# Two experts' token rows selected by one-hot products on TensorE in a two-layer transformer step on one Trainium2 core

## The reference, cut to what matters

```python
def hier_moe(h, w_rg_l, w_re_l, w_gate_l, w_up_l, w_down_l):
    grp_logits = jnp.einsum('btd,dg->btg', h, w_rg_l)              # 4 groups
    grp_idx = jnp.argmax(grp_logits, axis=-1)
    ...                                                            # the 4 experts of that group
    top_val, top_idx = lax.top_k(exp_logits, TOP_K)                # TOP_K = 2
    gates = ...                                                    # 16 experts, two not zero per token
    hidden = jax.nn.silu(jnp.einsum('btd,edf->btef', h, w_gate_l)) * jnp.einsum('btd,edf->btef', h, w_up_l)
    hidden = hidden * gates[..., None]
    return jnp.einsum('btef,efd->btd', hidden, w_down_l)           # f = 256, d = 1024
```

## Time and profile before

| what | value |
|---|---|
| median of 3 runs | 1436.62 us (1427.18 to 1441.4) |
| profiled execution, its own time | 1429.83 us |
| its span, first to last instruction | 1428.1 us |
| mean granted TensorE clock | 0.939 of 2.4 GHz |
| PE busy | 1253.6 us (88%) |
| DVE, ACT, POOL busy | 537.6, 378.2, 155.8 us |
| share of the ending chain on PE, DMA, DVE | 78%, 7%, 6% |

### The profile page before, as it was taken

How to read it: one execution, slowest core, us unless ns; L and a number is a source line. 1 busy time by engine, 2 the same in 40 slices (tenths; PEclk the granted TensorE clock), 3 DMA queues, 4 the chain that set the end, 5 groups by cost and what they waited for, 6 DMA issues and landing times.

```text
span 1428.1 us, 16575 instructions
## 1 busy us (share of the span) xinstructions
PE 1253.6 (88%) x5768; PEld 721.4 (51%) x5768; DVE 537.6 (38%) x1371; ACT 378.2 (26%) x963; POOL 155.8 (11%) x257
## 2 busy tenths in 40 slices
PE   4999897899999869999689998789999996999970
PEld 2455454465566545444355555456556653445430
DVE  0232264445565422112143415454546542111216
ACT  0121254434333101111021215453433310111111
POOL 3200210100000210000131102000000011000005
PEclk9999889999999979999899997999899997999995
DMA  9986635699111688999862143531001168799945
GB/s 347 391 303 215 239 127 196 239 365 327 64 59 60 248 310 320 370 364 369 296 234 88 65 159 127 207 120 65 32 31 59 60 243 324 285 365 369 365 188 221
DMA packets 125355, 314.75 MB, mean 220 GB/s; under 512 B 9520, under 2 KB 57936, under 8 KB 112608
## 3 DMA queue, kind: packets, MB, share of 16 engines
q1 hardware_dynamic: 90160, 240.50, 46.6%
q0 software_dynamic: 13072, 47.07, 8.8%
q10 hardware_dynamic: 22048, 26.22, 5.2%
HBM read 233.05 MB, written 80.71 MB: 220 GB/s over the span
## 4 chain that ended last, share of the span: by engine, by line
PE 78%; DMA 7%; DVE 6%; issue 3%; ACT 2%; SPq 2%; POOL 1%; ACTq 0%; POOLq 0%; DVEq 0%
PE ps L705 16%; PE ps L781 15%; PE ps L638 10%; PE ps L461 9%; PE ps L801 8%; PE ps L521 7%; DMA ring<-in_w_mod 4%; PE ps L480 3%; PE ps L542 3%; PE ps L466 2%; PE ps L728 2%; SPq L869 1%; DMA big<-in_x 1%; PE ps L596 1%; PE ps L507 1%
## 5 line engine op out<-in xcount | busy, mean ns | idle before, releaser
L705 PE MATMUL ps<-ring,big 128*128 128x384 f32 (+2 forms) x640 | 232.3, 522 | 3.9 <-ACT big L1157 3.9
L705 PEld LDWEIGHTS ps<-ring,big 128*128 128x128 f32 x640 | 121.1, 191 | 107.2 <-issue 64.7
L781 PE MATMUL ps<-ring,arena 128*128 128x512 f32 x384 | 169.1, 593 | 2.4 <-DVE arena L1899 2.4
L521 PE MATMUL ps<-arena 64*128 64x128 f32 (+5 forms) x576 | 142.5, 454 | 21.5 <-DVEq L1601 14.2
L461 PEld LDWEIGHTS ps<-consts,arena 128*128 128x128 f32 (+2 forms) x888 | 110.5, 160 | 77.1 <-issue 52.8
L461 PE MATMUL ps<-consts,arena 128*128 128x128 f32 (+2 forms) x888 | 134.5, 283 | 14.6 <-ACT arena L1073 6.4
L638 PE MATMUL ps<-ring,big 128*128 128x512 f32 x320 | 143.0, 598 | 2.4 <-DVE arena L1667 1.6
L1073 ACT ACTIVATE arena<-ps 128x384 f32<-128x384 f32 (+3 forms) x140 | 69.0, 493 | 242.2 <-PE ps L461 241.8
L521 PEld LDWEIGHTS ps<-arena 64*128 64x128 f32 (+1 forms) x576 | 82.3, 210 | 80.8 <-issue 68.1
L781 PEld LDWEIGHTS ps<-ring,arena 128*128 128x128 f32 x384 | 71.2, 190 | 83.4 <-issue 83.4
L638 PEld LDWEIGHTS ps<-ring,big 128*128 128x128 f32 x320 | 59.0, 190 | 72.4 <-issue 66.4
(11 more groups left out here) (197 smaller groups left out, 1386.0 us busy)
## 6 DMA issues: line engine op xcount, KB each, us to landing
ring<-in_w_mod SPq DMA_DIRECT2D x20, 2048.0 KB, 14.2
ring<-in_w_up SPq DMA_DIRECT2D x22, 1024.0 KB, 8.6
ring<-in_w_gate SPq DMA_DIRECT2D x22, 1024.0 KB, 5.8
slots<-zeros ACTq DMA_DIRECT2D x8, 2560.0 KB, 18.7
slots<-zeros SPq DMA_DIRECT2D x8, 2560.0 KB, 19.9
arena<-slots SPq DMA_DIRECT2D x32, 512.0 KB, 5.3
arena<-in_w_down SPq DMA_DIRECT2D x16, 1024.0 KB, 11.7
slots<-arena POOLq DMA_DIRECT2D x32, 512.0 KB, 9.3
```

Source lines behind the costliest of these rows:

```text
L521: mm = pe.matmul(two(2 * h)[:, at:at + hi - lo], queries(pr, h), keys(pr, h, lo, hi), start=(at % 512 == 0), stop=True, skip_group_check=True)
L705: mm = pe.matmul(ps[:, c, 0:CHUNKS[c][1]], hT[:, s, k, :], slot[c][:, k, 0:CHUNKS[c][1]], start=(k == 0), stop=(k == KD - 1))
L781: mm = pe.matmul(ps[:, b, :], xgT[:, b, k * P:(k + 1) * P], w_gu[q][:, :, k, :], start=(k == 0), stop=(k == KD - 1))
```

## The change

Experts 0 and 1 (`NEAR = 2`) no longer read `slots`. For each tile `near` takes a row's place within experts 0 and 1 out of the rank product, less 65536 if the row is theirs, and `one_hot` compares it with a table of 128 numbers for each expert, which gives a 128 x 128 matrix of zeros and ones (rows of the tile against places). `first_rows(L, e, i)` multiplies the tile's rows, as weights, with that matrix, and adds the five tiles up in PSUM: the sum is the transposed input of expert e, for which scatter, load and `x_turn` served before. All rows are still scattered, for experts 2 to 15 and for the overflow. The table is loaded into `gqa`, whose own content for the next layer is loaded once the matrices are made. The spin, both early `x_turn`, and the waits of PE for `scat_out` go; SP now loads the rows of experts 2 and 3 there. `place_rows` of the last tile moves behind the first `x_copy`, `total` goes to another bank and to the end of PE's list, and `up(1)` follows `up(0)` directly.

```diff
-PLACE = [6, 6, 6, 5, 4]
+PLACE = [6, 6, 6, 5, None]
+NEAR = 2
+FAR = 65536.0
...
                     if s - PROJ[i] == POS[i]:
                         rank(L, i)
                         if i == LAST:
-                            O.take(pe, ("total", L))
+                            first_rows(L, 1, 2)
+                            first_rows(L, 1, 3)
+                            first_rows(L, 0, LAST)
+                            first_rows(L, 1, LAST)
+                            M.take(pe, ("total", L))
...
+            def first_rows(L, e, i):
+                pe.wait_ge(oh_done, NEAR * (TILES * L + i) + e + 1)
+                pe.wait_ge(h_done, h2_no(L, i))
+                for k in range(KD):
+                    mm = pe.matmul(ps[:, first_bank(e)[k // 4], (k % 4) * P:(k % 4 + 1) * P], h2_rows(i)[:, k:D:KD],
+                                   oh[e][:, i * P:(i + 1) * P], start=(i == 0 and k % 4 == 0), stop=(i == LAST),
+                                   skip_group_check=True)
+                if i == LAST:
+                    mm.then_inc(e_xT, 1)
...
-                pe.wait_ge(scat_out, 160 * (L + 1))
-                spin(7, 9)
-                x_turn(0, 0, True)
                 up(0, 0, True)
-                x_turn(1, 1, False)
+                up(1, 1, True)
                 h_turn(0, 0, True)
-                up(1, 1, True)
                 x_turn(2, 0, False)
...
+                sp.wait_ge(e_xTa, E0 + 1)
+                half_up_load(2, 2, 1)
                 sp.wait_ge(scat_out, 160 * (L + 1))
-                for e in range(2):
-                    sp.dma_start(xg[:, e, :], slots[e * ROOM:e * ROOM + P, :]).then_inc(xg_in[e], 16)
-                half_up_load(2, 2, 1)
+                for e in range(NEAR, 4):
+                    sp.dma_start(xg[:, e % 2, :], slots[e * ROOM:e * ROOM + P, :]).then_inc(xg_in[e % 2], 16)
                 down_load(2, 2)
-                sp.wait_ge(O.full, O[("total", L)])
+                sp.wait_ge(M.full, M[("total", L)])
+                sp.wait_ge(idx_done, TILES * (L + 1))
                 up_load(3, 3)
                 down_load(3, 3)
...
+                pool.dma_start(gqa[:, :], t_in["near"].unsqueeze(0).broadcast_to([P, NEAR * P])).then_inc(room_in, 16)
...
                     if n == PLACE[i]:
+                        near(L, i)
                         place_rows(L, i)
+                        if i == LAST - 1:
+                            one_hot(L, i)
...
+            def near(L, i):
+                dve.wait_ge(O.full, O[("pos", L, i)])
+                go(STT(r_q[:, i, :], r_T[:, 0:NEAR], -FAR, ps[:, 6, 0:NEAR], ALU.mult, ALU.add))
+
+            def one_hot(L, i):
+                dve.wait_ge(room_in, 16 * (L + 1))
+                for e in range(NEAR):
+                    TS(oh[e][:, i * P:(i + 1) * P], gqa[:, e * P:(e + 1) * P], r_q[:, i, e:e + 1], None,
+                       ALU.is_equal).then_inc(oh_done, 1)
...
+                pick_sum(L, LAST)
+                x_copy(0, 0, True)
+                place_rows(L, LAST)
+                x_copy(1, 1, True)
```

More of the change, by code:

```diff
@@ L244, in program @@
         r_s, o = place(o, 2)
+        r_q, o = place(o, TILES, NEAR)
         gi, ei = r_gi.bitcast(U32), r_ei.bitcast(U32)
@@ L279, in rtile @@
             rt_at[0] += n
-            assert rt_at[0] <= A1
+            assert rt_at[0] <= A1 - 1024
             if len(dims) == 2:
@@ L330, in program @@
             "lg_done", "pick_done", "sum_done", "idx_done", "scat_out", "ctl_done"))
-        first_in = sem("first_in")
+        first_in, room_in, oh_done = (sem(n) for n in ("first_in", "room_in", "oh_done"))
         ew_in = [sem(f"ew{i}_in") for i in range(4)]
@@ L355, in turn_bank, with first_bank @@
             return (S[1], 2) if (i, half) == (LAST, 0) else (M, 7)
+        def first_bank(e):
+            return (1, 3) if e == 0 else (4, 5)
         def route_bank(i):
@@ L601, in ranks @@
                         if i == LAST:
-                            O.take(pe, ("total", L))
-                            pe.wait_ge(sum_done, TILES * (L + 1))
-                            pe.matmul(ps[:, 6, 0:NE], ones, r_sum[:, i, :], start=True, stop=True,
-                                      skip_group_check=True).then_inc(O.full, 1)
+                            first_rows(L, 1, 2)
[3 more added lines that the diff above has]
+                            M.take(pe, ("total", L))
+                            pe.wait_ge(sum_done, TILES * (L + 1))
+                            pe.matmul(ps[:, 7, 0:NE], ones, r_sum[:, i, :], start=True, stop=True,
+                                      skip_group_check=True).then_inc(M.full, 1)
+            def first_rows(L, e, i):
[7 more added lines that the diff above has]
+                    mm.then_inc(e_xT, 1)
             def beside(L, s):
@@ L615, in beside @@
                             pe.matmul(ps[:, 4, 0:RW], h2T[:, k * P:(k + 1) * P], wr[:, k, :], start=(k == 0), stop=False)
+                        first_rows(L, 0, 0)
                     for half in range(2):
@@ L641, in beside @@
                     if n == ROUTE[i] and i == LAST:
+                        first_rows(L, 0, 1)
                         pe.wait_ge(M.free, M.freed[("h2", L, i, 1)])
@@ L646, in beside @@
                         mm.then_inc(T.full, 1)
+                        first_rows(L, 0, 2)
+                        first_rows(L, 0, 3)
+                        pe.wait_ge(T.free, T.freed[("rt", L, i)])
+                        first_rows(L, 1, 0)
+                        first_rows(L, 1, 1)
             def turn_entry(L, i):
@@ L1249, in x_copy @@
                     act.wait_ge(e_xT, E0 + e + 1)
-                    act.activation(xgT[:, b, 0:512], ps[:, 4, :], ACT.Copy).then_inc(e_xTa, 1)
+                    bank = first_bank(e)[0] if early else 4
+                    act.activation(xgT[:, b, 0:512], ps[:, bank, :], ACT.Copy).then_inc(e_xTa, 1)
                 def silu(e, b):
@@ L1262, in _ @@
                 x_copy(0, 0, True)
+                x_copy(1, 1, True)
                 silu(0, 0)
-                x_copy(1, 1, True)
                 silu(1, 1)
@@ L1440, in _ @@
                 if L < DEPTH - 1:
+                    pool.wait_ge(oh_done, NEAR * TILES * (L + 1))
                     vector_loads(L + 1)
@@ L1708, in pick, with pick_sum @@
                 elif L:
-                    dve.wait_ge(O.full, O[("total", L - 1)])
+                    dve.wait_ge(M.full, M[("total", L - 1)])
                 go(STT(r_T, cst["expert"], r_ix[:, 2:3], r_oh[:, 0, :], ALU.is_equal, ALU.add))
                 dve.sem_inc(pick_done, 1)
+            def pick_sum(L, i):
                 TS(r_oh[:, 1, :], cst["expert"], r_ix[:, 2:3], None, ALU.is_equal)
@@ L1751, in beside @@
                         TT(h2_rows(i), heads[:, i, :], rowA2[:, kind, :], ALU.mult).then_inc(hA_done, 1)
+                        if i == LAST - 1:
+                            for j in range(LAST - 1):
+                                one_hot(L, j)
                     if n == ROUTE[i]:
@@ L1755, in beside @@
                         pick(L, i)
+                        if i < LAST:
+                            pick_sum(L, i)
                         dve.wait_ge(hA_done, norm_no(L, 2, i))
                         STT(h2_rows(i), h2_rows(i), rsd[:, i:i + 1], rowB2[kind], ALU.mult, ALU.add).then_inc(h_done, 1)
+                        if i == LAST:
+                            near(L, i)
+                            one_hot(L, i)
             dve.wait_ge(const_in, 16)
@@ L1855, in _, with x_copy, gate, hid_copy @@
                 attention(L, 4)
+                E0 = NE * L
+                def x_copy(e, b, early):
+                    if not early:
+                        dve.wait_ge(e_h, E0 + e - 1)
+                    dve.wait_ge(e_xT, E0 + e + 1)
+                    bank = first_bank(e)[1] if early else 5
+                    dve.tensor_copy(xgT[:, b, 512:1024], ps[:, bank, :]).then_inc(e_xTd, 1)
+                def gate(e, b):
+                    dve.wait_ge(e_sg, E0 + e + 1)
+                    TT(hid[:, b, :], sg[:, b, :], ps[:, b, FF:2 * FF], ALU.mult).then_inc(e_hid, 1)
+                def hid_copy(e, b, early):
+                    dve.wait_ge(e_hT, E0 + e + 1)
+                    if not early:
+                        dve.wait_ge(e_d, E0 + e - 1)
+                    dve.tensor_copy(hidT[:, b, :], ps[:, 6, 0:FF]).then_inc(e_hTe, 1)
+                def y_copy(e, b, early):
+                    dve.wait_ge(e_d, E0 + e + 1)
+                    if not early:
+                        dve.wait_ge(ys_out[b], 8 * E0 + 8 * (e - b))
+                    dve.tensor_copy(yb[:, b, 512:1024], ps[:, 3, :]).then_inc(e_yd, 1)
                 go(TT(r_gd, r_lg[:, :, 0:4], r_g8[:, :, 0:1].broadcast_to([P, TILES, 4]), ALU.subtract))
@@ L1860, in _ @@
                 dve.sem_inc(rx2, 1)
-                dve.wait_ge(O.full, O[("total", L)])
```

(10 more changed lines are left out.)

6 lines of the change are left out of this document (2 added, 4 removed).

## The result

The changed kernel takes 1461.26 us (median of 4 runs, 1455.31 to 1465.59) against 1434.43 us for the kernel before (4 runs): ratio 1.0185, 95% interval 1.012 to 1.025, so 17 to 36 us slower. I had forecast 1419 us. Its profiled execution took 1465.59 us (span 1463.8).

A forecast was written before the change was run, and what follows sets the result against it. PE, busy 88% of the span, was taken as the bound. Gains of 4.85 + 7.1 + 2 x 1.77 = 15.5 less costs of 0.9 gave 14.6 us less: 1415.2 profiled, 1419 against the mean of 1433.8; range 1409 to 1436.

The forecast's parts named there:

- the price of `first_rows`: On PE, ten `first_rows` per layer before the first `up`: 1.80 us each, range 1.70 to 1.98, 18.0 in sum.
- The rule that I set aside: For weight reads of `first_rows`: each access crossing to a new 16-byte line pays a penalty, slowing all 80 products a layer.
- The slower rival: In `first_rows` on PE: a record costs 0.21 to 0.23 us, so 21 us slower, 1455; chance 0.10.
- no overlap: In `first_rows` on PE: weight load and product do not run at once, so one takes 3.4 to 3.6 us.
- a lower clock: PE's clock falls to 1.2 GHz during `first_rows`, as at 499, so one takes 3.4 to 3.6 us.
- The rest of PE's list: Before the first `up`: router product 1.70, four transposes 0.45, rank 0.35, total 0.13 us; with `first_rows`, 20.6.
- Fed without a wait: Between router product and first `up`, picks and `one_hot` are ready before PE asks; PE's list alone sets the start, 514.8.
- `near`: In front of `place_rows` in each tile: 0.27 us, 0.54 for the third tile over both layers, 0.36 for the first two.
- The rivals on transfers: At the experts, transfers hold PE up: rows of expert 2 come late, chance 0.13, or DMA sets the pace, chance 0.08.
- The forecast of 27.4 us from the router product to SP's issue of the rows: Scatter for expert 2 done and SP free at 27.4 us; loads landed at 31.1 to 32.4, PE wants them at 34.8.
- late rows: At `x_turn(2)`: scatter and load exceed the slack of 2.4 to 3.7 us; gain 6.6, so 1427; chance 0.13.
- the DMA bound: In the steady run of the experts: DMA sets the pace, experts starting earlier only wait longer, 1430 to 1434; chance 0.08.

The follow-up runs named there:

- dense version: The changed kernel with `first_rows` reading its weights as 128 adjacent floats instead of every eighth one: 1421.28 us beside 1429.24 of the kernel before.
- dense version that is right in all outputs: The changed kernel with adjacent floats in `first_rows` and gate and up weights of experts 0 and 1 loaded in fitting order: 1420.83 us, ratio 0.9919 to the kernel before.

## Why the prediction was wrong, step by step

- **The failed step: the price of `first_rows`.** I wrote "I take 1.80, since columns, weights and stride are the same", from eight transposes in 0.90. It was 3.83 on average (38.3 us for ten), 2.03 too much, ten times in each of two layers: 40.6 us, which turns 14.6 us less into 26.0 more. The transpose was the nearest row in shape, but it is another operation: its record stayed at 0.1125 us with the step, where a product's went from 0.113 to 0.239. The durations of the loads, 192 ns with the step and 140 without, were in the trace of the kernel before and would have given the hint; I compared only the distances between starts.
- **The rule that I set aside.** The sentence "By the row they cost nothing, and the row counts" was the wrong verdict: the row was one of transposes and could not answer for products. The note on cachelines in the Trainium skill (SBUF — State Buffer, section "Door 1: The DMA port swizzle") had the sign right; it gives no price.
- **The slower rival was the right one in place, sign and nearly in price:** I put a record at 0.21 to 0.23, and the total at 1455; it was 0.239, and 1461. Of the causes that I wrote for it, no overlap and a lower clock were both wrong: the dense version takes 0.113 a record with the same columns, and the clock was 1.00. That its number came out close is luck; only the rule set beside it named the cause. With 0.10 it had too small a chance.
- **The rest of PE's list was right.** Router halves 0.81 each, not 0.85; transposes 0.44, rank 0.37, total 0.14. With dense weights the sum is 20.68 in both layers, against 20.6 forecast, and the two `up` with `h_turn` take 14.05, against 14.20.
- **Fed without a wait: right,** in the changed kernel and in the dense one.
- **`near`: right in place, smaller.** In the kernel after PE waits 0.62 us for the third tile's placing instead of 0.43, 0.19 rather than 0.27. In layer 1 it is 0.43 and 0.62 again. The costs of `near` on the first two tiles are too small to be told apart here.
- **The rivals on transfers did not come.** `x_turn(2)` never waits, in the changed kernel nor in the dense one, and the experts run at 11.4 us each in all of them, so DMA was no bound. The forecast of 27.4 us from the router product to SP's issue of the rows was met in the dense version: 521.02 - 493.82 = 27.2.
- **The range** ended at 1436: it took in late rows and the DMA bound and left out the slower rival at 1455, the number that came nearest.

## What to carry to other kernels

Price a new product by a row of a product, not of a transpose, and look at the step in its weights: here a float32 product whose 128 weight columns lie in 128 different 16-byte lines took 0.235 to 0.239 us a record, twice the 0.113 of adjacent ones. Where PE has to be fed with every k-th element, let the layout of the other operand (here the order in which the weights are loaded) make the elements adjacent. And a filler that replaces idle PE time pays only up to the length of the wait: 20.7 us of work in a gap of 25 to 28 won 5 to 7 us per layer, 40.9 us of it lost 13 to 15.

## What the runs showed of the hardware that was not expected

- The weight load of a 128 x 128 float32 product takes 192 ns in the trace for adjacent floats, 196, 261, 330 and 335 ns for steps of two, three, four and eight; the record takes 0.113, 0.119, 0.175, 0.235 and 0.239 us. A fit to these is 1.84 ns per 16-byte line touched, where this exceeds 0.113 us.
- The same step in the weights of a transpose costs its record nothing, 0.1125 us with a step of eight and 0.112 without, though its load takes 192 ns instead of 140.
- Loads of 1 MB in pieces of 1 KB instead of 8 KB delayed nothing here: in the dense version that is right in all outputs both first products start without a wait, the first 20.68 us after the router product, as with pieces of 8 KB.
